# A decoder step on one core: the key turns of the sample group come after the forget gates and the query copies, and a broadcast load moves ahead

## What is computed

```
z = rms_norm(h) @ w_in                 # -> ... q, k, v, forget logits fz ...
logf = log_sigmoid(fz + b_forget)
rev  = reverse_cumsum(logf_past) - logf_past                     # over the cached tokens
sp   = q . k_past / sqrt(64) + cumsum(logf)[q] + rev[k_past]     # 8 heads, 4096 cached keys
sn   = q . k / sqrt(64) + cumsum(logf)[q] - cumsum(logf)[k]      # the 4 new tokens, causal
p    = softmax(concat(sp, sn));  out = p_past @ v_past + p_new @ v
```

## Time and profile before

| | us |
|---|---|
| median of 3 runs | 2086.73 |
| lowest and highest of them | 2084.26, 2095.47 |
| the profiled execution's own time | 2084.26 |
| its span in the trace | 2082.4 |
| PE busy | 1897.4 (91%) |
| DVE busy | 832.2 (40%) |
| ACT busy | 443.0 (21%) |
| POOL busy | 262.7 (13%) |
| transfers, mean over the span | 220 GB/s |

### The profile page before, as it was taken

The page is one execution under the profiler, slowest core; times in us unless marked ns, Lnnn a source line. Parts: engine busy times, 40 slices in busy tenths (PEclk is TensorE's granted clock), DMA queues, the critical chain, the costliest instruction groups (busy, mean ns, idle before and its releaser), DMA issues.

```text
span 2082.4 us, 33477 instructions
## 1 busy us (share of the span) xinstructions
PE 1897.4 (91%) x12402; PEld 1123.6 (54%) x12402; DVE 832.2 (40%) x1867; ACT 443.0 (21%) x1021; POOL 262.7 (13%) x402
## 2 busy tenths in 40 slices
PE   6998987888879999999999989995999999999994
PEld 4676654455458868888884467643333333333331
DVE  5643456777555623333326324435111111111115
ACT  3111124433400101111111123231222222222223
POOL 0202323323400000000000000000111111111110
PEclk9999999999979999999999999997999999999997
DMA  7659999998741122102112204019899999999966
GB/s 270 230 180 325 343 328 329 349 331 312 256 170 51 51 93 70 51 11 61 51 36 78 71 33 152 21 59 340 280 383 384 376 373 377 375 375 370 368 242 255
DMA packets 207018, 458.55 MB, mean 220 GB/s; under 512 B 18625, under 2 KB 48338, under 8 KB 206730
## 3 DMA queue, kind: packets, MB, share of 16 engines
q1 hardware_dynamic: 174282, 357.89, 48.2%
q0 software_dynamic: 32576, 98.53, 13.7%
HBM read 432.44 MB, written 32.17 MB: 223 GB/s over the span
## 4 chain that ended last, share of the span: by engine, by line
PE 70%; DMA 10%; DVE 7%; issue 5%; ACT 3%; SPq 2%; POOLq 2%; DVEq 1%; POOL 0%; ACTq 0%
PE ps L1274 17%; PE ps L1570 11%; PE ps L1601 6%; PE ps L1325 5%; PE ps L1581 5%; PE ps L1354 5%; DMA kraw<-in_cache_k 3%; DMA vpage<-in_cache_v 3%; PE ps L1610 3%; PE ps L1075 3%; PE ps L1443 2%; DVE kt L2098 2%; PE ps L1103 2%; PE ps L1118 2%; POOLq L824 1%
## 5 line engine op out<-in xcount | busy, mean ns | idle before, releaser
L1570 PE MATMUL ps<-gu,xgT 128*64 128x512 f32 x1024 | 226.8, 595 | 0.9 <-ACT xgT L1915 0.9
L2098 DVE STREAM_TRANSPOSE kt<-kraw 128x1024 f32<-128x1024 f32 x128 | 151.2, 1220 | 78.7 <-DMA kraw<-in_cache_k 70.4
L2926 POOL DMA_DIRECT2D vpage<-in_cache_v x232 | 124.7, 537 | 307.5 <-issue 289.0
L1274 PE MATMUL ps<-xnT,ring 128*128 128x264 f32 x672 | 161.4, 391 | 0.9 <-issue 0.9
L2814 DVE TENSOR_TENSOR sig_a<-ps,sig_a 128x256 f32<-128x256 f32 x32 | 13.6, 425 | 324.1 <-ACT sig_a L1919 324.1
L1274 PEld LDWEIGHTS ps<-xnT,ring 128*128 128x128 f32 x672 | 129.1, 193 | 25.4 <-issue 3.1
L1570 PEld LDWEIGHTS ps<-gu,xgT 128*64 128x64 f32 x1024 | 70.5, 137 | 132.0 <-issue 128.9
L1601 PE MATMUL ps<-wd,hidT_a 128*64 128x512 f32 x512 | 116.9, 598 | 19.7 <-ACT hidT_a L1925 9.9
L1581 PE MATMUL ps<-gu,xgT 128*32 128x512 f32 x1024 | 115.8, 592 | 0.0
L1103 PE MATMUL ps<-xnT,early 128*128 128x352 f32 x320 | 101.9, 474 | 4.2 <-DVE xnT L2042 4.2
L1226 PE MATMUL ps<-vpage,sprobT 128*32 128x512 f32 x464 | 66.7, 645 | 21.8 <-DMA vpage<-in_cache_v 21.7
(11 more groups left out here) (441 smaller groups left out, 2963.2 us busy)
## 6 DMA issues: line engine op xcount, KB each, us to landing
kraw<-in_cache_k SPq DMA_DIRECT2D x256, 256.0 KB, 4.9
gu<-in_w_expert_gate SPq DMA_DIRECT2D x32, 2048.0 KB, 20.3
gu<-in_w_expert_up SPq DMA_DIRECT2D x32, 2048.0 KB, 24.9
wd<-in_w_expert_down SPq DMA_DIRECT2D x31, 2048.0 KB, 21.2
vpage<-in_cache_v POOLq DMA_DIRECT2D x232, 256.0 KB, 4.8
ring<-in_w_in SPq DMA_DIRECT2D x12, 1024.0 KB, 8.8
yy<-y_d SPq DMA_DIRECT2D x16, 512.0 KB, 10.5
early<-in_w_in SPq DMA_DIRECT2D x6, 1024.0 KB, 10.3
```

What stands on the lines that cost most here:

```text
L1274: last = nc.tensor.matmul(bank(R.bank(name, f, q))[:, 0:QT], weight[:, k], src[:, k, cols], start=k == 0, stop=k == HK - 1)
L1570: last = nc.tensor.matmul(bank(0)[h * BA:(h + 1) * BA, :].rearrange("p (x n) -> p x n", x=2), src[:, k, 0:BA], weight[:, k, :, h * DE // 2 ...
L2098: last = nc.vector.transpose(kt[n % 2].rearrange("p c e s -> p (c e s)")[:, x * 1024:(x + 1) * 1024], kraw[n % 2].rearrange("p c d -> p (c ...
L2926: pool.dma_start(vpage[value_place(n)][:, p, :], t["cache_v"][ds(page, 1)].rearrange("a s d -> (a s) d")).then_inc(v_in[value_place(n)], 16)
```

## The change

On DVE, the forget logits move to the front, directly behind the cached gates; all preparations (`qnew`, `tops`, `qblk`, `sums`, then the query copies) follow them, and `turn_keys(0)` and `turn_keys(1)` come last, right at the head of the loop. The wait for the k columns ahead of `turn_keys(0)` goes, since the wait for "fz", which PE makes after them, now stands before. On SP, `load_rev(0)` moves from behind unit 3 to ahead of unit 2, with its wait for `rev_stored`.

```diff
             load_unit(0), load_unit(1)
             sp.dma_start(xn_d, xnT).then_inc(xn_stored, 16)
+            sp.wait_ge(rev_stored, 16 * 8)
+            load_rev(0)
             for n in range(2, NSU):
                 sp.wait_ge(kt_ready, n - 1)
                 load_unit(n)
-                if n == 3:
-                    sp.wait_ge(rev_stored, 16 * 8)
-                    load_rev(0)
...
             dve.sem_inc(after_ready, 1)
+            R.made(dve, "fz")
+            for g in range(4):
+                last = nc.vector.tensor_scalar(lf[:, 0, ...], bank(R.bank("fz"))[...], convp[...], None, ALU.add)
...
+            nc.vector.memset(qnew, 0.0)
+            nc.vector.memset(tops, NEG)
             for p in range(2):
                 nc.vector.memset(qblk[p], 0.0)
+            nc.vector.memset(sums, 0.0)
+            dve.drain()
             dve.wait_ge(qk_ready, 1)
-            for g in range(4):
-                for r in range(4):
-                    nc.vector.tensor_copy(qgrp[...], qs[...])
-            dve.drain()
-            spread_queries(0)
-            R.made(dve, "k", KC - 1, COLS - 1)
-            turn_keys(0), turn_keys(1)
-            R.made(dve, "fz")
...
             for c in range(KC):
                 for half in range(2):
                     ... qnew[rows, c, :, at_:at_ + DS] <- qs[rows, c, :] ...
-            dve.drain()
+            for g in range(4):
+                for r in range(4):
+                    nc.vector.tensor_copy(qgrp[...], qs[...])
+            dve.drain()
+            spread_queries(0)
             dve.sem_inc(side_ready, 1)
...
+            turn_keys(0), turn_keys(1)
             for n in range(NSU + LAG):
```

More of the change, by code:

```diff
@@ L2080, in _ @@
             dve.sem_inc(after_ready, 1)
-            def spread_queries(b):
-                for g in range(4):
[L2084 to L2087, removed]
-                dve.drain()
[L2090 to L2105, removed]
-                for r in range(4):
-                    nc.vector.tensor_copy(qgrp[g * 32:(g + 1) * 32, :, r % 2, r // 2, :], qs[r * 32:(r + 1) * 32])
-            dve.drain()
-            spread_queries(0)
-            R.made(dve, "k", KC - 1, COLS - 1)
-            turn_keys(0), turn_keys(1)
             R.made(dve, "fz")
@@ L2119, in _, with spread_queries @@
                                            ).then_inc(abs_ready, 1)
+            def spread_queries(b):
+                for g in range(4):
+                    rows = slice(g * 32, (g + 1) * 32)
+                    nc.vector.tensor_copy(
+                        qblk[b % 2].rearrange("p e (x q g) -> p e x q g", x=3, g=4)[rows, :, 0:3:2, :, g],
+                        qgrp[rows, :, :, :, b * DS:(b + 1) * DS].rearrange("p j e x q -> p (j e) x q"))
+                dve.drain()
             nc.vector.memset(qnew, 0.0)
             nc.vector.memset(tops, NEG)
+            for p in range(2):
+                nc.vector.memset(qblk[p], 0.0)
             nc.vector.memset(sums, 0.0)
             dve.drain()
+            dve.wait_ge(qk_ready, 1)
             for c in range(KC):
@@ L2128, in _ @@
                                           qs[rows, c, :].rearrange("p (b q) -> p b q", b=DB))
+            for g in range(4):
+                for r in range(4):
+                    nc.vector.tensor_copy(qgrp[g * 32:(g + 1) * 32, :, r % 2, r // 2, :], qs[r * 32:(r + 1) * 32])
             dve.drain()
+            spread_queries(0)
             dve.sem_inc(side_ready, 1)
@@ L2205, in take_prompt, with turn_keys @@
                                         ).then_inc(R.by["dve"], 1)
+            def turn_keys(n):
+                if n >= NSU:
+                    return
+                dve.wait_ge(k_in[n % 2], 64 * (n // 2 + 1))
+                if n >= 2:
+                    R.made(dve, "sq", n - 2)
+                for x in range(2):
+                    last = nc.vector.transpose(kt[n % 2].rearrange("p c e s -> p (c e s)")[:, x * 1024:(x + 1) * 1024],
+                                               kraw[n % 2].rearrange("p c d -> p (c d)")[:, x * 1024:(x + 1) * 1024])
+                last.then_inc(kt_ready, 1)
             def join_scores(n):
```

## The result

| | before | changed |
|---|---|---|
| median of 8 runs each, us | 2085.85 | 2106.42 |
| lowest and highest | 2083.84, 2095.47 | 2099.07, 2111.88 |
| the profiled execution's own time | 2084.26 | 2089.49 |
| its span | 2082.4 | 2087.5 |

The ratio on record is 1.008 with a 95% interval of 1.0056 to 1.0103, which on 2086 us is +12 to +21 us: slower, as forecast. The two medians alone differ by 20.6 us, a ratio of 1.0099; ten further executions of the changed kernel are on record, and the median of all nineteen is 2103.61 us. So the forecast of 2102 is off by 4 us against the median of the table and by less against the ratio. The profiled execution is the fastest of the nineteen, so its span shows less of the loss than the median. Its head, though, shows a delay of the forecast size.

A forecast was written before the change was run, and what follows sets the result against it. PE's own work sets the pace from 72 to 160 us, the pages much of it from 160 to 560. 14.8 (gap) + 2.5 (clock) - 1.0 (rev load) = +16.3 us, forecast 2102 us, range 2095 to 2109.

The forecast's parts named there:

- PE's gap is DVE's work behind the wait for fz: Ahead of the first score product, PE waits for all of DVE's preparation behind fz: 14.8 us of idle time.
- The copies' length: Sixteen qgrp copies on DVE take 4.3 us instead of 6.82, since POOL's issues of rev_d stores had held them.
- two held copies: Within the qgrp copies' 4.3 us, two holds of 0.4 us for POOL's issues of value pages.
- The rival of 6.82 us: The qgrp copies keep their length through strided access, not POOL: 2.5 us more, 18.8 in all; chance 0.15.
- The clock: Behind PE's idle time the granted clock restarts at the lower level: +2.5 us, bounds 1.5 and 3.5.
- The rival of a further spell of low clock in the page stretch: Low clock also at further waits of the page stretch: 2.6 us more, 18.9 in all; chance 0.14.
- The give-back of 1.0 us by the rev load: The earlier rev load removes PE's wait for the v columns: -1.0 us, bounds 0 and -1.07.
- one wait in one execution: PE's wait of 1.07 us for the v columns in the first profile, at the end of the chain of waits.
- Nothing catches up: Page loads, xnT reload and weights are released by PE's or DVE's progress, so the +16.3 us stays.
- The absorption rival: Page transfers run on while PE stands and its page waits shrink, by up to 16.3 us; chance 0.14, part or whole.
- The sign that I had named, the reload of xnT: Its start, 573.29 us before, moves by the same 16 us; under 10 us with the gap there means wrong.

The follow-up runs named there:

- 5.74: The changed kernel with the memsets and query copies done ahead of the wait for fz; ratio 1.0049 to the kernel before.
- 17.25: The kernel before with nothing moved, but 15 memsets and a drain each ahead of the first turn of keys; ratio 1.0102.
- 32.66 us of idle time: The changed kernel with 15 more memsets behind the forget logits, also called the doubled gap; ratio 1.0175 to the kernel before.
- DVE's order alone: The changed kernel with the rev load back behind unit 3; ratio 1.0096 to the kernel before.
- once the stores were away: The kernel before with POOL's stores of rev_d held back until PE made the third k product; one run, 2095.24 us.
- PE is kept busy: The changed kernel with 22 more products of 352 columns on PE in the gap; ratio 1.0073 to the kernel before.
- second profile of the kernel before: The kernel before run once more with no edit, and profiled; ratio 1.0001.

## Why the prediction was right, point by point

**PE's gap is DVE's work behind the wait for fz: right.** Predicted 14.8 us later, measured 13.9. In this execution fz ended 0.7 us sooner (70.47 against 71.15 us), so the fairer pair is from fz's end to the first score product: 85.8 - 71.15 = 14.65 predicted, 14.36 us measured. The copies took 3.73 us where I had put 4.3; the other terms were together 0.3 us longer. That 2102 us is met so closely is partly luck, since the interval is 10 us wide. The experiments with 5.74, 17.25 and 32.66 us of idle time show the loss following the gap, and the one with DVE's order alone shows where it comes from.

**The copies' length: right in its reading, slightly too long.** The pairing with POOL's stores of `rev_d` was the cause (3.63 us once the stores were away). I added two held copies for POOL's issues of value pages; these hold next to nobody (the longest `qgrp` copy beside them took 240 ns, and one `qnew` copy 263 ns against a median of 176). The rival of 6.82 us falls.

The prediction took from the Trainium skill ("SBUF — State Buffer", "SBUF: two separate sides") the case in which VectorE's copy has the shared port pair and GpSimd can't write its descriptors. In these runs the copies lengthened, and POOL's issues took 7.13 and 7.14 us with and without them. The same section gives the pair to whichever of the two starts first, so this case fits it too. That it was the port pair which held the copies, no run here shows.

**The clock: right.** +2.5 predicted, 2.4 measured at the head (2.0 to 2.9 over the kernels with a gap), and gone when PE is kept busy. The rival of a further spell of low clock in the page stretch is not seen: PEclk from 160 to 560 us was 0.95 before and 0.95 after. It is not excluded either. The second profile of the kernel before has 0.94, the edited kernels have 0.93 to 0.95, and 0.01 in the clock of a stretch of 400 us can be up to 4 us.

**The give-back of 1.0 us by the rev load: wrong.** It rested on one wait in one execution. The same program run again does not show it, the rev load alone gains 0.2 us by unit 10, and the fall of the shift from 16.2 to 14.3 us in the changed kernel, which looks like that give-back, comes without the rev load's move as well. The prediction also called the wait at the v columns all that there was, and passed over a wait of 0.42 us of PE at line 1215 in the same trace:

```profile
89.27 0.46 PE L1215 MATMUL ps<-sraw,consts 128*32 128x128 f32 x8 [0.42 <-ACT sraw L1707]
```

There the rev load's move does help when it stands alone: its run has no such wait. In the changed kernel the wait is gone with or without the rev load's move, since PE comes late itself. In the second profile of the kernel before 11.38 us pass from unit 2 to unit 3, in every kernel with a gap 10.9. That is the 0.5 in the sum of the head: 13.6 + 2.4 - 0.5 = 15.5 us by unit 10 against the second profile, not 16.3 with a term of -1.0.

**Nothing catches up: right.** The absorption rival, to which I gave 0.14, asked for page transfers that run on while PE stands. The doubled gap costs its full length, within an interval of 5 us each way. The sign that I had named, the reload of xnT, is the weaker evidence: it moved by 16.7 us against one profile of the kernel before and by 10.2 against the other.

**What stays open.** The losses lie 1 to 5 us above the shifts at unit 10 in all seven kernels with an edit. Each alone is within its interval, and the kernels of one set share the same runs of before, so I don't read a cause into it. Nor is the width of the page stretch (374 to 387 us between units 10 and 63 over the profiles, one program giving 374 and 382) traced further. The low time of the changed kernel's profiled execution is explained only in part: from unit 10 to unit 63 it took 374.5 us, the short end, and it was 9 to 12 us quicker behind the start of the reload than the two profiles of the kernel before, which was not traced.

No kernel here beats the kernel before. The rev load's move alone gave nothing that these runs can tell from zero: -1 to +10 us.

## What to carry to other kernels

When a wait is moved up a queue, price everything that stands behind it up to the instruction that another engine needs: that sum, not the wait, is the new idle time. Hidden work is free only at its place. A wait of about 1 us in a single profile is not yet a term of a sum; look whether a second execution has it. And an idle time of TensorE has a second price in the clock behind it, which here was 1.7 to 2.9 us for idle times from 1.94 to 32.66 us and did not follow their length.

## What the runs showed of the hardware that was not expected

- POOL's stores of 128x8x32 elements to `rev_d` (0.89 us per issue) stretched DVE's copies beside them from 0.22 to as much as 0.71 us each; its loads of value pages (2.30 us for four issues) stretched one `qnew` copy by 0.09 us and hardly any other. The copies were short again (217 to 223 ns) as soon as the issues ended, when none of the stores had landed yet.
- PE's idle time of 5.74 us cost nearly the same by the clock behind it as 14.36 us: 2.2 and 2.4 us between the shifts of unit 0 and unit 1. Even 1.94 us of it brought the granted clock to 0.53 and cost 1.7 us; behind waits of 0.25 and 0.42 us at the same place it stayed at 1.00.
